# Output projections of a two-block kernel: one 512-column matmul for both halves of the activations, and a VectorE sum of the bank's halves

## The reference, cut to what matters

```python
for layer in range(DEPTH_2):            # 2 layers
    ...
    mix = jnp.concatenate([y_conv.astype(h.dtype), y_ret], axis=-1)    # 256 x 2048
    out = jnp.einsum("bse,ed->bsd", mix, w_out[layer])                 # 2048 x 1024
    x = x + rms_norm(out, post_norm[layer]).astype(x.dtype)
```

## Time and profile before

| | |
|---|---|
| timed runs | 949.75, 951.6, 953.24 us; median 951.6 us |
| span of the profiled execution | 949.0 us; its device time is not listed beside it |
| instructions | 21,725 |
| TensorE matmul busy | 916.4 us (97%), 7684 matmuls |
| VectorE, ScalarE, GpSimd busy | 598.6 (63%), 498.1 (52%), 691.2 (73%) us |
| output projection, layer 1 | 643.53 to 687.06 us of the span |
| output projection, layer 2 | 892.08 to 935.60 us of the span |

### The profile page before, as it was taken

The page is one execution under the profiler, slowest core; times in us unless marked ns, Lnnn a source line. Parts: engine busy times, 40 slices in busy tenths (PEclk is TensorE's granted clock), DMA queues, the critical chain, the costliest instruction groups (busy, mean ns, idle before and its releaser), DMA issues.

```text
span 949.0 us, 21725 instructions
## 1 busy us (share of the span) xinstructions
PE 916.4 (97%) x7684; PEld 896.8 (94%) x7684; DVE 598.6 (63%) x1122; ACT 498.1 (52%) x820; POOL 691.2 (73%) x898
## 2 busy tenths in 40 slices
PE   5998999999999999999999999999999999999996
PEld 5887999999999999999999999999989999999996
DVE  3889889767776444523566567774366566877522
ACT  3555655575567665555554455445455444544451
POOL 1786587687769877887676758888857667788873
PEclk9999999999999999999999999999999999999998
DMA  9976567654545557554544435655525444455521
GB/s 360 417 300 238 223 225 272 258 185 171 178 175 182 188 211 260 200 190 177 179 155 156 177 133 187 212 183 208 188 89 179 152 158 159 155 213 186 202 86 45
DMA packets 28225, 185.22 MB, mean 195 GB/s; under 512 B 3027, under 2 KB 5504, under 8 KB 6272
## 3 DMA queue, kind: packets, MB, share of 16 engines
q1 hardware_dynamic: 25832, 167.93, 48.9%
q10 hardware_dynamic: 2328, 16.40, 4.8%
HBM read 183.26 MB, written 1.07 MB: 194 GB/s over the span
## 4 chain that ended last, share of the span: by engine, by line
PE 86%; DVE 8%; issue 2%; ACT 2%; DMA 1%; SPq 0%; POOL 0%; ACTq 0%; POOLq 0%; DVEq 0%
PE mm L609 25%; PE mm L611 25%; PE mm L610 25%; PE mm L643 1%; ACT w_hi L1109 1%; DVE ada_raw L1563 1%; DVE w_lo L1525 1%; DVE score L1683 1%; PE ps_o L991 1%; PE ps_s L974 1%; DMA hot<-onehot 1%; PE ps_o L1065 1%; PE mm L627 1%; PE mm L628 1%; PE mm L629 1%
## 5 line engine op out<-in xcount | busy, mean ns | idle before, releaser
L526 POOL TENSOR_TENSOR w_lo<-raw,w_hi 128x256 fp32r<-128x256 f32 x880 | 680.9, 808 | 235.3 <-ACT w_hi L1109 235.2
L609 PE MATMUL mm<-u_hi,w_hi 128*128 128x256 f32 x1568 | 447.2, 285 | 0.5 <-ACT w_hi L1109 0.3
L610 PE MATMUL mm<-u_lo,w_hi 128*128 128x256 f32 x1568 | 435.7, 278 | 0.0
L611 PE MATMUL mm<-u_hi,w_lo 128*128 128x256 f32 x1568 | 435.5, 278 | 0.0
L1109 ACT ACTIVATE w_hi<-raw 128x1024 fp32r<-128x1024 f32 x291 | 307.6, 1058 | 160.0 <-PE mm L611 150.0
L609 PEld LDWEIGHTS mm<-u_hi,w_hi 128*128 128x128 f32 x1568 | 295.7, 189 | 5.8 <-issue 4.9
L610 PEld LDWEIGHTS mm<-u_lo,w_hi 128*128 128x128 f32 x1568 | 295.8, 189 | 2.0 <-issue 1.9
L611 PEld LDWEIGHTS mm<-u_hi,w_lo 128*128 128x128 f32 x1568 | 295.9, 189 | 0.0
L1525 DVE TENSOR_TENSOR w_lo<-raw,w_hi 128x1024 fp32r<-128x1024 f32 x71 | 95.6, 1346 | 64.3 <-ACT w_hi L1109 54.4
L609 PE MATMUL mm<-h_hi,w_hi 128*128 128x256 f32 x256 | 70.8, 277 | 0.0
L610 PE MATMUL mm<-h_lo,w_hi 128*128 128x256 f32 x256 | 70.7, 276 | 0.0
(11 more groups left out here) (350 smaller groups left out, 1323.8 us busy)
## 6 DMA issues: line engine op xcount, KB each, us to landing
raw<-weights SPq DMA_DIRECT2D x145, 1024.0 KB, 4.8
ada_raw<-ada ACTq DMA_DIRECT2D x14, 1024.0 KB, 5.4
ada_raw<-ada SPq DMA_DIRECT2D x6, 1024.0 KB, 9.5
ada_more<-ada SPq DMA_DIRECT2D x4, 1024.0 KB, 12.1
bias<-tab_scratch SPq DMA_DIRECT2D x1, 1536.0 KB, 9.4
dec<-decay ACTq DMA_DIRECT2D x1, 1536.0 KB, 7.0
x<-xT SPq DMA_DIRECT2D x1, 1024.0 KB, 10.7
out<-x SPq DMA_DIRECT2D x4, 256.0 KB, 2.3
```

Of the source, the lines that this page charges most:

```text
L526: ins = nc.gpsimd.tensor_tensor(lo[:, at], r[:, at], hi[:, at], ALU.subtract)
L609: nc.tensor.matmul(dst, wh, rhs_hi(k), start=a, stop=False)
L610: nc.tensor.matmul(dst, wh, rhs_lo(k), start=False, stop=False)
L611: i = nc.tensor.matmul(dst, wl, rhs_hi(k), start=False, stop=b)
```

## The change

The tiles of high and low activations become one tile with an index for the half: `mix` is 128 x 2 x 16 x 256, with `mix_hi = mix[:, 0]` and `mix_lo = mix[:, 1]`. The same is done with `u`, `h`, `oa`, `ob`, `oc` and `m`; the halves of each stood side by side in SBUF already, so addresses stay as they are. For the units of the output projection with j in `WIDE_OUT` (0 to 6), a step of `unit` issues two matmuls in place of three (`two`): the high weights by a moving operand of 2 x 256 columns, high and low activations, into all 512 columns of the bank, and the low weights by the high activations into columns 0 to 255. The product is then the sum of the bank's two halves. VectorE makes it (`tensor_reduce` over a view in which the halves are innermost) into PSUM, in `out_sum[j % 2]`, releases the bank by `taken`, and ScalarE squares and scales `out_sum` instead of the bank. Block 7 and all other units issue the same three matmuls as before (`three`, `three_apart`). In `diff` form, without the places that only pass the joined tile on:

```diff
+WIDE_OUT = range(KC - 1)
...
-    mix_hi = p3("mix_hi", [P, 2 * KC, T], F32R)
-    mix_lo = p3("mix_lo", [P, 2 * KC, T], F32R)
+    mix = p3("mix", [P, 2, 2 * KC, T], F32R)
+    mix_hi, mix_lo = mix[:, 0], mix[:, 1]
...
     c_out = [ps_s[1][:, T * e:T * e + T] for e in range(2)]
+    out_sum = [ps_s[0][:, 0:T], ps_t[:, 0:T]]
...
+        def three(dst, wh, wl, both, first, last):
+            return three_apart(dst, wh, wl, both[:, 0, :], both[:, 1, :], first, last)
+        def two(bank, wh, wl, both, first, last):
+            nc.tensor.matmul(bank[:, :], wh, both, start=first, stop=False)
+            return nc.tensor.matmul(bank[:, 0:T], wl, both[:, 0, :], start=False, stop=last)
+        def three_apart(dst, wh, wl, hi, lo, first, last):
+            nc.tensor.matmul(dst, wh, hi, start=first, stop=False)
+            nc.tensor.matmul(dst, wh, lo, start=False, stop=False)
+            return nc.tensor.matmul(dst, wl, hi, start=False, stop=last)
...
-                    nc.tensor.matmul(dst, wh, rhs_hi(k), start=a, stop=False)
-                    nc.tensor.matmul(dst, wh, rhs_lo(k), start=False, stop=False)
-                    i = nc.tensor.matmul(dst, wl, rhs_hi(k), start=False, stop=b)
+                    if wide:
+                        i = two(mm[oo % 4], wh, wl, both(k), a, b)
+                    elif apart is None:
+                        i = three(dst, wh, wl, both(k), a, b)
+                    else:
+                        i = three_apart(dst, wh, wl, *apart(k), a, b)
...
                 unit(None, uA + 64 + n, oA + 64 + j,
-                     (lambda off: lambda k: mix_hi[:, off + k, :])(off),
-                     (lambda off: lambda k: mix_lo[:, off + k, :])(off), ready=rd, first=q == 0, last=q == 1)
+                     (lambda off: lambda k: mix[:, :, off + k, :])(off), ready=rd, first=q == 0, last=q == 1, wide=j in WIDE_OUT)
...
                 if q == 1:
                     o = oA + 64 + j
-                    square_x(3 + 2 * l, j, mm[o % 4][:, 0:T])
-                    A(o_out[:, j, :], mm[o % 4][:, 0:T], ACT.Identity, scale=col("post", KC * l + j))\
-                        .then_inc(taken[o % 4], 1)
+                    if j in WIDE_OUT:
+                        act.wait_ge(taken[o % 4], o // 4 + 1)
+                        src = out_sum[j % 2]
+                    else:
+                        src = mm[o % 4][:, 0:T]
+                    square_x(3 + 2 * l, j, src)
+                    A(o_out[:, j, :], src, ACT.Identity, scale=col("post", KC * l + j))\
+                        .then_inc(S["out_kept"] if j in WIDE_OUT else taken[o % 4], 1)
                 high(None, c + SLOTS)
...
                 dve.wait_ge(S["unit_done"], c + 1)
+                if q == 1 and j in WIDE_OUT:
+                    o = oA + 64 + j
+                    if j >= 2:
+                        dve.wait_ge(S["out_kept"], len(WIDE_OUT) * l + j - 1)
+                    V.tensor_reduce(out_sum[j % 2], mm[o % 4][:, :].rearrange("p (e t) -> p t e", e=2), AX.X, ALU.add)\
+                        .then_inc(taken[o % 4], 1)
                 if (j, q) == (1, 1) or q == 0 and j >= 2:
                     add_square(n_out, j - 1)
...
             dve.wait_ge(S["x3_ready"], KC)
+            dve.wait_ge(S["out_kept"], len(WIDE_OUT) * (l + 1))
```

More of the change, by code:

```diff
@@ L145, in _build @@
     keep("step_u", [P, 8])
-    u_hi = keep("u_hi", [P, KC, T], F32R)
-    u_lo = keep("u_lo", [P, KC, T], F32R)
+    u_both = keep("u_both", [P, 2, KC, T], F32R)
+    u_hi, u_lo = u_both[:, 0], u_both[:, 1]
     keep("step_raw", [P, 8])
@@ L585, in low_ready, with unit @@
                 pe.wait_ge(S["lo_dve" if c % 4 == 3 else "lo_pool"], lin(g, per_c, c + 1))
-        def unit(g, c, o, rhs_hi, rhs_lo, ready=None, parts=1, first=True, last=True, turn=(8, 2), w=T):
+        def three(dst, wh, wl, both, first, last):
[7 more added lines that the diff above has]
+            return nc.tensor.matmul(dst, wl, hi, start=False, stop=last)
+        def unit(g, c, o, both, ready=None, parts=1, first=True, last=True, turn=(8, 2), apart=None, wide=False, w=T):
             u_hi_, u_lo_ = rounded(g, c)
@@ L626, in first_units @@
                     wh, wl = w_hi[:, s, k * P:(k + 1) * P], w_lo[:, s, k * P:(k + 1) * P]
-                    nc.tensor.matmul(dst, wh, hi[:, k, 0:w], start=k == 0, stop=False)
-                    nc.tensor.matmul(dst, wh, lo[:, k, 0:w], start=False, stop=False)
-                    i = nc.tensor.matmul(dst, wl, hi[:, k, 0:w], start=False, stop=k == KC - 1)
+                    if apart is None:
+                        i = three(dst, wh, wl, u_both[:, :, k, :], k == 0, k == KC - 1)
+                    else:
+                        i = three_apart(dst, wh, wl, *apart(k), k == 0, k == KC - 1)
                     if k == KC - 1:
@@ L712, in first_step @@
             dst = first_bank[c][:, 0:T]
-            nc.tensor.matmul(dst, hi[:, at], u_hi[:, k, :], start=k == 0, stop=False)
-            nc.tensor.matmul(dst, hi[:, at], u_lo[:, k, :], start=False, stop=False)
-            i = nc.tensor.matmul(dst, lo[:, at], u_hi[:, k, :], start=False, stop=k == KC - 1)
+            i = three(dst, hi[:, at], lo[:, at], u_both[:, :, k, :], k == 0, k == KC - 1)
             if k == KC - 1:
@@ L854, in _ @@
             elif c >= 6:
-                unit(None, c, c, uh, ul)
+                unit(None, c, c, uu)
             if c == 6:
@@ L926, in _ @@
         pe.wait_ge(S["shift_lo"], 3)
-        first_units(2, U_F1, O_F1, early_ready, hi=ua_hi, lo=ua_lo, behind=behind_early, w=U_WIDE)
+        without = lambda k: (ua_hi[:, k, 0:U_WIDE], ua_lo[:, k, 0:U_WIDE])
+        first_units(2, U_F1, O_F1, early_ready, apart=without, behind=behind_early, w=U_WIDE)
         for i in range(2, EARLY):
-            unit(None, U_F1 + i, O_F1 + i, lambda k: ua_hi[:, k, 0:U_WIDE], lambda k: ua_lo[:, k, 0:U_WIDE], w=U_WIDE)
-        unit(None, U_F1 + EARLY, O_F1 + EARLY, uh, ul, ready=u_ready(1))
+            unit(None, U_F1 + i, O_F1 + i, None, apart=without, w=U_WIDE)
+        unit(None, U_F1 + EARLY, O_F1 + EARLY, uu, ready=u_ready(1))
         for i in range(EARLY + 1, 8):
-            unit(None, U_F1 + i, O_F1 + i, uh, ul)
+            unit(None, U_F1 + i, O_F1 + i, uu)
         with pe.Fori(0, 3) as g:
             for i in range(8):
-                unit(g, U_F1 + 8 + i, O_F1 + 8 + i, uh, ul)
+                unit(g, U_F1 + 8 + i, O_F1 + 8 + i, uu)
         with pe.Fori(0, 2) as g:
@@ L942, in _ @@
                         pe.wait_ge(S["hl_ready"], KC * (q + 1))
-                    unit(g, U_F2 + 4 * j + q, O_F2 + j, lambda k: h_hi[:, q * KC + k, :],
-                         lambda k: h_lo[:, q * KC + k, :], first=q == 0, last=q == 3, turn=(16, 1))
+                    unit(g, U_F2 + 4 * j + q, O_F2 + j, lambda k: h_both[:, :, q * KC + k, :], first=q == 0, last=q == 3, turn=(16, 1))
                     if j == 0 and q == 0:
@@ L1020, in first_turn @@
                     elif i >= n:
-                        unit(None, c0 + i, o0 + i, uh, ul)
+                        unit(None, c0 + i, o0 + i, uu)
                     if i == row_at:
@@ L1039, in turn @@
                 for i in range(8):
-                    unit(g, c0 + i, o0 + i, uh, ul)
+                    unit(g, c0 + i, o0 + i, uu)
                     if i == 1:
@@ L1071, in _ @@
             for i in range(8):
-                unit(None, uA + 32 + i, oA + 32 + i, uh, ul)
+                unit(None, uA + 32 + i, oA + 32 + i, uu)
                 if i == 0:
```

38 lines of the change are left out of this document (19 added, 19 removed).

## The result

| | before | after |
|---|---|---|
| executions | 20 | 20 |
| median | 953.36 us | 959.67 us |
| lowest, highest | 949.39, 961.61 us | 953.68, 964.31 us |
| ratio, 95% interval | | 1.005 (1.0026 to 1.0075) |

The kernel became slower, by about 0.5%, where 950.0 us and no measurable change were forecast. The quotient of the two medians is larger, 1.0066, because the executions of both kernels lie in two clusters: of the 20 of before, 14 lie from 949.4 to 954.2 us and six from 959.5 to 961.6, with none between. The ratios here leave out two executions that were over 1.5% above the fastest of their kernel (one of before, 964.09 us, and one of experiment 4); the counts of executions take them in. The change costs in two places.

A forecast was written before the change was run, and what follows sets the result against it. TensorE's matmul pace was taken to bound the output projections; 224 steps winning 7.1 ns each gave -1.6 us, VectorE's sum and the rest nothing, so 950.0 us against 951.6 (-0.17%), range 948.0 to 952.6.

The forecast's parts named there:

- What bounds the stage: Both output projections: TensorE's own pace sets them, matmuls filling all of both stretches at granted clock 1.00.
- The wide matmul's price: Output projections: a 512-column float32r matmul taken at 215 ns, from float32 records; 226.8 if the pace went by columns.
- The narrow matmul's price: Output projections: the 256-column matmul behind a wide one taken at 118 ns, against 113.4 in the steady stream.
- columns at the second pace: Rival, output projections: all columns at the slower pace, 3 x 118 = 354 ns a step, 3.1 us lost, 954.7 us; chance 0.05.
- The sum -1.6 us: Whole kernel: 224 steps in the output projections each win 7.1 ns (333 for 340.1), all else at nothing.
- VectorE's sum: Output projections: 14 new reductions of 0.69 us each; ScalarE about 0.75 us later, the delay hidden, no cost.
- slack of GpSimd: Layer 1's projection: GpSimd ends 1.9 us before TensorE needs its work; 0.9 us stays after the change.
- The passage at nothing: Behind each projection's last unit: last block stays narrow, so square, running sum, variance and dummies start as before; no cost.
- Range: Whole kernel: 948.0 to 952.6 us, leaving out the slower rivals and the best tail.

The follow-up runs named there:

- experiment 4: Kernel after, each unit with its eight wide matmuls first and then its eight narrow ones instead of alternating; 953.47 us, ratio 0.9995, projection 44.27 us.
- experiment 8: Kernel after with one wide matmul at the start of each block 0 to 6, narrow ones otherwise; one execution, projection 45.22 us.
- experiment 12: Kernel before with one float32 matmul of 512 columns ahead of each output projection; one execution, 383 projection matmuls in 45.11 us, 117.8 ns each.
- Experiment 2: Kernel after with three narrow matmuls back in all blocks, VectorE's 512-element reduction kept; 952.22 us, ratio 0.9989 to before.
- Experiment 9: Kernel before with 8 dummy matmuls (1.8 us) ahead of layer 1's output projection; 958.43 us, ratio 1.0063.
- experiment 5: Kernel before with 4 and 6 more dummy matmuls in the passage between the layers; 950.92 us, ratio 0.9978.
- experiment 6: Kernel after with 4 and 6 more dummy matmuls in the passage between the layers; 954.90 us, ratio 1.0005.
- experiment 11: Kernel before with more dummies between the layers and the head norms' eight 512-column float32 matmuls each split into two of 256; 951.08 us, ratio 0.9976.

## Why the prediction was wrong

- **What bounds the stage: right.** TensorE alone; no wait of it in either projection.
- **The wide matmul's price: the step that failed.** I took 215 ns from the float32 rows for a float32r matmul of 512 columns. It takes 235 (226 when first, 231 and 236 in turn when in a row: experiment 4). Over 224 matmuls these 20 ns are 4.5 us, nearly all of the way from the forecast -1.6 to the measured +3.4. A float32 record of 512 column times is no measure of a float32r one of 512 columns. The Trainium skill ("TensorE: Matmul & The Clock Gate", Back-to-back issue gap) gives N / 2.4 + 2.5 ns for the isolated gap, which makes 215.8 and 109.2 ns, an estimate. This case's trace does not agree with it for float32r at either width: 235 and 118 ns, or 226 and 113.
- **The narrow matmul's price: right, for a reason that I did not see.** 118 ns was taken from the earlier trace rows as something that a narrow matmul pays behind a long one. It is a pace that one long matmul can set for hundreds of float32r matmuls (experiments 8 and 12), and the wide ones run at it too. With the earlier trace rows in hand I applied it to one of three 256-column parts of a step; it holds for all three: 3 x 118 = 353. The rival "columns at the second pace", given 0.05, had the mechanism and its size: 3.1 us forecast, 3.4 measured, the rest being that all 16 units pay and not 14. That the sum took 118 for the narrow one was luck in part: the number was right, and its use in one place of three was not.
- **The sum -1.6 us became +3.4 us.** Forecast were 224 x 7.1 ns won; measured were 2 x 1.70 us lost.
- **VectorE's sum: right.** 0.69 forecast, 0.70 measured; square 0.78 late; slack of GpSimd 1.7 us with the slower TensorE, 0.9 forecast with the faster. Experiment 2 shows its whole cost as none.
- **The passage at nothing: wrong.** I wrote that what is behind the last unit starts as before. It does, but later in time, and the clock's fall there, some 6 to 9 us each time, comes in 12 of 20 executions where it came in 20 of 87. Experiment 9 shows that 1.8 us of dummies ahead of the projection make it as frequent, at the fast pace. Experiments 5, 6 and 11 show that it stays away when the passage's idle time is filled. I had read the clock only inside the stages, and not asked what spread the three timed runs; 20 runs of before reach from 949 to 962. Only one shift was tried; what other shifts do, and why a shift matters, is open.
- **Range.** It ended at 952.6; even the undisturbed 955.2 is above. The bound by columns at the second pace, 954.7, was left out of it on its small chance.

No kernel here that computes the whole product beats before beyond its interval. The two with filled passages, 5 and 11, come nearest (0.9978 and 0.9976): no long fall of the clock in 24 executions.

## What to carry to other kernels

Price a matmul of a new length only by rows of the same type; per column, float32r has nothing to win from longer moving operands here, since what it pays over 2.4 GHz grows with the columns. When a trace shows two paces for the same instruction, find what switches them before costing either, since one long matmul in a dense stream can slow all that follow, and look in several executions: the same stretch of unchanged code can run at either. Where a kernel's runs fall into two clusters, look at the granted clock of each before reading a median, and fill TensorE's idle gaps before moving work about in front of them. Read a small change by the length of the stage that it touches, not by the total.

## What the runs showed of the hardware that I had not expected

- float32r matmuls of 256 columns run at 113.3 or at 118 ns, start to start, both at a granted clock of 1.00. The slow pace outlasts its cause: 383 matmuls behind one float32 matmul of 512 columns (experiment 12), and the last 94 narrow ones of a projection behind a last wide float32r one (experiment 8). Where the kernel has such float32 matmuls and two of 256 columns stood in the place of each, the fast pace was back after five (experiment 11). But narrow ones came back after one behind eight wide ones in a row (experiment 4), 23 in a row were slow behind short float32 matmuls, and 527 in one execution and not in another behind a wait. What sets and releases the pace is open.
- A float32r matmul of 512 columns costs as much as two of 256: 226 ns at the fast pace (the first), 235 at the slow (2 x 113, 2 x 118).
- Fewer weight loads won nothing: the kernel after has 224 fewer, and a first wide matmul, with one load, takes the 226 ns of two narrow ones with two. Whether a load gates a narrow one was not tested.
- The clock's fall between the layers came in 20 of 87 executions of the kernel before, in 7 of 12 with 1.8 us of dummies ahead of the projection, and in 0 of 36 with the passage's gaps filled (long falls, by the mean clock of the execution).
